# Attention that takes its token tiles in reverse: first the two with 512 keys, then the two context tiles with 256 keys

## The reference, cut to what matters

```python
def latent_attention(q, k, v, kc, vc):
    kk = jnp.concatenate([k, kc], axis=1)      # 512 keys
    vv = jnp.concatenate([v, vc], axis=1)
    ...
    def block(qblk):                           # 128 queries
        s = jnp.einsum('bqkgd,bmkd->bkgqm', qblk, kk).astype(jnp.float32) * scale
        p = jax.nn.softmax(s, axis=-1).astype(vv.dtype)
        return jnp.einsum('bkgqm,bmkd->bqkgd', p, vv)

def context_attention(qc, kc, vc):             # 256 keys
    s = jnp.einsum('blkgd,bmkd->bkglm', qg, kc).astype(jnp.float32) * ATT_HEAD_DIM ** -0.5
    p = jax.nn.softmax(s, axis=-1).astype(vc.dtype)
    o = jnp.einsum('bkglm,bmkd->blkgd', p, vc)
```

## Time and profile before

| | us |
|---|---|
| median of 3 runs | 4459.85 |
| the three runs | 4431.76, 4459.85, 4463.53 |
| the profiled execution, its own time | 4434.76 |
| its span, first to last instruction | 4432.9 |
| PE busy | 4021.8 (91% of the span) |
| DVE busy | 2656.9 (60%) |
| ACT busy | 1804.5 (41%) |
| mean granted clock of TensorE | 0.932 |

### The profile page before, as it was taken

How to read it: one execution, slowest core, us unless ns; L and a number is a source line. 1 busy time by engine, 2 the same in 40 slices (tenths; PEclk the granted TensorE clock), 3 DMA queues, 4 the chain that set the end, 5 groups by cost and what they waited for, 6 DMA issues and landing times. The chain is left out here.

```text
span 4432.9 us, 70375 instructions
## 1 busy us (share of the span) xinstructions
PE 4021.8 (91%) x27702; PEld 3578.6 (81%) x27702; DVE 2656.9 (60%) x5280; ACT 1804.5 (41%) x3615; POOL 0.2 (0%) x4
## 2 busy tenths in 40 slices
PE   7798966999999999999999999889857899987999
PEld 4366555879999699999997899757547899977999
DVE  0313566336885957777668766512365578768666
ACT  1013123225555754544546544401214455555443
POOL 0000000000000000000000000000000000000000
PEclk8896977999999999999999999889568999999999
DMA  4120310225565446656554565412003456532665
GB/s 153 48 76 20 105 46 27 95 77 152 182 183 171 124 147 181 183 181 182 183 182 128 146 182 183 159 57 93 0 1 104 136 176 181 181 108 68 183 181 165
DMA packets 142194, 568.32 MB, mean 128 GB/s; under 512 B 15808, under 2 KB 17344, under 8 KB 130240
## 3 DMA queue, kind: packets, MB, share of 16 engines
q1 hardware_dynamic: 142016, 566.14, 41.1%
HBM read 565.03 MB, written 1.05 MB: 128 GB/s over the span
## 5 line engine op out<-in xcount | busy, mean ns | idle before, releaser
L1030 ACT ACTIVATE high<-ring 128x512 fp32r<-128x512 f32 x1632 | 1028.9, 632 | 1192.3 <-PE ps L489 607.8
L1398 DVE TENSOR_TENSOR low<-ring,high 128x512 fp32r<-128x512 f32 x1632 | 1090.3, 690 | 432.6 <-ACT high L1030 416.5
L878 PE MATMUL ps<-wt,high 128*128 128x256 f32 x6144 | 1116.2, 284 | 8.2 <-DVE low L1398 8.2
L489 PE MATMUL ps<-h2hi,high 128*128 128x256 f32 x3456 | 984.2, 285 | 26.9 <-DVE low L1398 26.9
L489 PE MATMUL ps<-h2lo,high 128*128 128x256 f32 x3456 | 979.6, 283 | 0.0
L489 PE MATMUL ps<-h2hi,low 128*128 128x256 f32 x3456 | 979.6, 283 | 0.0
L878 PEld LDWEIGHTS ps<-wt,high 128*128 128x128 f32 x6144 | 958.6, 192 | 8.7 <-issue 5.7
L878 PE MATMUL ps<-wt,low 128*128 128x256 f32 x3072 | 871.6, 284 | 0.0
L489 PE MATMUL ps<-arena 128*128 128x128 f32 (+6 forms) x2800 | 521.3, 347 | 212.6 <-ACT arena L1030 108.1
L489 PEld LDWEIGHTS ps<-h2hi,high 128*128 128x128 f32 x3456 | 665.1, 192 | 27.8 <-DVE h2lo L1398 12.7
L489 PEld LDWEIGHTS ps<-h2lo,high 128*128 128x128 f32 x3456 | 665.2, 192 | 0.0
(11 more groups left out here) (150 smaller groups left out, 3447.1 us busy)
## 6 DMA issues: line engine op xcount, KB each, us to landing
ring<-u_in SPq DMA_DIRECT2D x384, 512.0 KB, 3.6
ring<-v_in SPq DMA_DIRECT2D x384, 512.0 KB, 3.6
ring<-win_in SPq DMA_DIRECT2D x56, 1024.0 KB, 4.8
ring<-wmod_in SPq DMA_DIRECT2D x24, 1024.0 KB, 4.9
ring<-wq_in SPq DMA_DIRECT2D x48, 512.0 KB, 3.6
ring<-wmod_in SPq DMA_DIRECT2D x48, 512.0 KB, 3.6
ring<-wbr_in SPq DMA_DIRECT2D x16, 768.0 KB, 4.3
ring<-wout_in SPq DMA_DIRECT2D x8, 1024.0 KB, 4.8
```

The costliest lines, as they stand in the source:

```text
L489: return pe.matmul(o, l_, r, start=first, stop=last)
L878: i = pe.matmul(o, w[:, k, :], wt[:, v % 2, b, :], start=first and j % 2 == 0 and w is w_hi and b == 0, stop=False, skip_group_check=True)
L1030: return act.activation(o, i_, f, **kw_)
L1398: return dve.tensor_tensor(o, a, b, op)
```

## The change

The list of tiles is reversed on PE, ACT and DVE: layer 0 takes 3, 2, 1, 0 and layer 1 takes 3, 2. The tile that was finished before the one at hand is therefore `t + 1` instead of `t - 1`, and the last one is `tiles[-1]`. Nothing else changes: no instruction is added or removed, and each engine issues as many of each kind as before.

```diff
@@ tensor
-                att = [(t, h) for t in outs(l) for h in range(AH)]
+                tiles = outs(l)[::-1]
+                att = [(t, h) for t in tiles for h in range(AH)]
...
-                    if h == 1 and t != outs(l)[0]:
-                        turn_out(t - 1)
-                turn_out(outs(l)[-1])
+                    if h == 1 and t != tiles[0]:
+                        turn_out(t + 1)
+                turn_out(tiles[-1])
@@ scalar
-                    if h == 2 and t != outs(l)[0]:
-                        copy_out(t - 1)
-                copy_out(outs(l)[-1])
+                    if h == 2 and t != tiles[0]:
+                        copy_out(t + 1)
+                copy_out(tiles[-1])
@@ vector
-                    if h == 0 and t != outs(l)[0]:
-                        divide(t - 1)
-                divide(outs(l)[-1])
+                    if h == 0 and t != tiles[0]:
+                        divide(t + 1)
+                divide(tiles[-1])
```

## The result

The changed kernel takes 4459.7 us, median of 20 runs (4457.95 to 4462.52). The kernel before took 4434.92 us, median of 20 runs of its own (4431.76 to 4463.58). The ratio is 1.004, with a 95% interval of 1.0026 to 1.0055; it agrees with the ratio of the means (4460.1 to 4442.2 us). The ratio of the two medians is higher, 1.0056, because the runs of before lie on two levels: 14 of the 20 between 4431.8 and 4436.0 us, and 6 between 4459.2 and 4463.6. All 20 runs after the change lie on the upper one. The change is clear of noise and small: 18 us between the means, 25 us between the medians.

The account below looks back on a forecast made before the run. PE was taken to bound attention of layer 0, at a time set by the clock. +0.5 (start) + 28.2 (lost rise) − 0.7 (drain) = +28.0 us on the profiled 4434.8 gave 4462 us; 8-in-10 range 4428 to 4468 us.

Parts of the forecast that it names:

- What bounds attention: Attention of layer 0: PE bounds it, DVE and ACT don't; its time depends on which heads fall under which clock.
- Step 1: Start of layer 0 attention: first `turn_p` at 377.17 us instead of 376.68, as the first two `scores` take longer; +0.5 us.
- Step 2: 512-key heads at the start of layer 0: 4.65 us each at clock 0.50 as in layer 1, no rise at tile 3's turn-out.
- Step 3: Context heads at the end of layer 0 attention: no rise of the clock, 2.51 us each as before.
- Steps 4 and 5: Layer 0 attention: 13 512-key heads lose full clock, 28.2 us; the drain of a 256-key tile gives −0.7 us.
- How this stands to the runs: Timed runs before: one with the rise, two without, so the median already pays the forecast time; +0.05% against 4459.85 us.
- Rival A: Layer 0: the clock rises at the turn-out of tile 3, near 425.5 us; 4432 to 4450 us, chance 0.13.
- Rival B: Start of layer 0 attention: 512-key heads placed first raise the clock at once; 4412 us, chance 0.04.
- Rival C: `mod_row` work behind layer 0 attention, 466 to 600 us: low clock carried into SSD; 4520 us, chance 0.02.
- Rival D: Order makes no difference to the clock; the rise comes as often at some other place; 4432 to 4463 us, chance 0.06.

## Why the prediction was right, and where it was off

*What bounds attention* held. The 27.8 us are all in PE's busy time, and DVE and ACT have none of it. The mechanism that was forecast, a rise of the clock in attention of layer 0 that no longer comes, is what the trace shows.

*Step 1, the start, +0.5 us.* DVE's step ahead of attention came 0.46 us later in this execution (368.14 against 367.68). The first `turn_p` came 0.96 us later (377.64 against 376.68), so the step itself cost 0.50.

*Step 2, layer 1 as the model.* The `turn_p` ahead of the turn-out of tile 3 was foretold for 422.01 us; with the 0.46 us of this execution that is 422.47, and it came at 422.48. The clock stayed low there, as in layer 1. But layer 1 was a less safe model for this than the step takes it to be: a delay of 1.7 us, which leaves program and surroundings as they are, brought the rise at this very place in 6 of 10 runs. That it didn't come without the delay rests on where the turn-out fell in time, which the prediction didn't weigh; in this the step had some luck.

*Step 3, context heads at 2.51 us*: as foretold, with three turn-outs among or behind them (456.61, 477.57 and 491.95 us) and no rise.

*Steps 4 and 5, the loss and the drain.* Attention ended at 493.90 us against 466.39, 27.5 us later, of which 0.46 are not its own. The sum had 28.0 and the measured is 27.05. The old order with the moved turn-out, which never rose, parts the two steps. From its first `turn_p` to DVE's first step after attention it takes 117.77 us:

```profile
373.70 0.66 PE L661 MATMUL ps<-kept,arena 128*128 128x128 f32 x2 [2.31 <-ACT arena L1030]
...
491.47 0.62 DVE L1577 COPY arena<-ps 128x128 f32<-128x128 f32 x2 [2.19 <-PE ps L489]
```

The kernel before takes 89.71 us for the same (466.39 − 376.68) and the changed one 116.26 (493.90 − 377.64). So the lost rise costs 28.06 us, where 28.2 was foretold, and the drain gave back 1.51 instead of the 0.7 that I took; the bound from above was 2.14. The span grew by 27.8 us, so what follows attention added 0.3, near the nothing that was taken.

*How this stands to the runs: the step that was off.* There are two levels, and their distance is the price of the rise; but I set the median run of before on the upper level, because two of three timed runs were there. In 20 runs 14 were on the lower one. So it isn't true that the change takes away "a chance of 28 us, not a time that the median has": it costs 25 us between the medians and 0.4% by the ratio, where +0.05% was foretold. The predicted 4462 us and the 4459.7 measured are 2 us apart in spite of this, since the 4462 was added up from the profiled execution, which was on the lower level, and not from the median. How often the old order reaches the lower level isn't fixed either: 14 of 20, 7 of 29, 11 of 13 and 12 of 13 in the four sets of runs. The last three sets were taken on three different chips, so the chip may set the share; nothing here tests it.

*Rival A* (a rise at the turn-out of tile 3, 4432 us) came in none of the 20 runs. It became true with a delay of 1.7 us (4437 us in 6 of 10 runs) and with a longer dense piece (4436). *Rival B*'s 4412 us is what attention costs at full clock from its start in layer 0 (4412.48 measured), but 512-key heads don't bring that about. It takes denser work ahead of them. That the two numbers agree so closely is luck: in this kernel the extra matmuls also run past the waits, and its first `turn_p` comes 15.90 us after the last transposes ahead of the decay sums, against 12.85 in the changed kernel. *Rival C* didn't come: from 494 to 600 us the clock is 0.94. *Rival D*, that the order doesn't matter to the clock, falls with the 20 runs on one level. The rule of the Trainium skill that the prediction weighed ("TensorE: Matmul & The Clock Gate", Part 1: sustained matmul activity releases the throttle) agrees with the dense matmuls of these runs (the longer piece, the filled waits) and not with the ordinary run of heads, 116.84 of 118.90 us busy at 0.50.

What stays open: what makes a time favourable, and what fixes the share of runs on the lower level for the old order, which differed between the sets. The traces have one execution of it, on that level; that its upper level is attention without the rise is shown for the delayed and the moved-turn-out kernel only, and taken over from them. Nor do the runs say in full why the kernel with the first six matmuls alone lies 2.7 us under the changed one. In the traced executions its first `turn_p` comes 1.8 us earlier (375.80 against 377.64 us in layer 0), as the scores ahead of it run at full clock.

## What to carry to other kernels

Where PE is busy with small matmuls, or with matmuls of 64 rows, look at the granted clock of the stretch before the order of the work: here the busy share was 98% and the clock half. A kernel whose times lie on two levels may owe it to one piece of dense work that comes at a favourable time or doesn't. Then a reordering, or 2 us of delay just ahead of it, can change how many runs lie on which level (from 14 of 20 to none, from none of 20 to 6 of 10) though the work is the same. Take the level of the kernel before from many runs: three of them put its median on the wrong one here. Filling PE's short waits ahead of such a stretch with matmuls that nobody reads gave 1.3% here; size them to the wait.

## What was not expected of the hardware

Eight matmuls in waits of 5.4 and 2.3 us kept attention at full clock in both layers, but six in the first wait alone didn't, in nine of ten runs: in the traced one a wait of 2.88 us was enough to lose the clock, and 115 us of nearly full PE busy time didn't win it back. Where the two matmuls cut that wait to 0.88 us, the clock stayed. Transposes of 128x128 in fp32 raised the clock as well as matmuls did (4436.35 against 4436.39 us, 10 of 10 runs each).
